# A relative-bias table built from 128 shifted copies of each row in DRAM, in a one-core decoder trunk

## What is computed

```python
for i in range(DEPTH):                       # DEPTH = 2
    y = swiglu(rms_norm(h, g[0]), ffn_w_gate[i, 0], ffn_w_up[i, 0], ffn_w_down[i, 0])
    h = h + 0.5 * rms_norm(y, g[1])
    u = rms_norm(h, g[2])
    y = nsa_mixer(u, ..., rel_bias) if i % 2 == 0 else fox_mixer(u, ...)
    h = h + rms_norm(y, g[3])
    y = swiglu(rms_norm(h, g[4]), ffn_w_gate[i, 1], ffn_w_up[i, 1], ffn_w_down[i, 1])
    h = h + 0.5 * rms_norm(y, g[5])
```

## Time and profile before

| | |
|---|---|
| median of 3 runs | 1093.38 us |
| profiled execution, its own time | 1094.15 us |
| its span | 1092.4 us |
| PE busy | 1062.8 us, 97% |
| DVE, ACT, POOL busy | 574.5, 482.5, 104.4 us |
| bytes moved by DMA | 187.79 MB |
| sub-layer 0 (first FFN) | about 0 to 217 us |

### The profile page before, as it was taken

The page is one execution under the profiler, slowest core; times in us unless marked ns, Lnnn a source line. Parts: engine busy times, 40 slices in busy tenths (PEclk is TensorE's granted clock), DMA queues, the critical chain, the costliest instruction groups (busy, mean ns, idle before and its releaser), DMA issues.

```text
span 1092.4 us, 18174 instructions
## 1 busy us (share of the span) xinstructions
PE 1062.8 (97%) x7545; PEld 973.8 (89%) x7545; DVE 574.5 (53%) x645; ACT 482.5 (44%) x613; POOL 104.4 (10%) x206
## 2 busy tenths in 40 slices
PE   6999999999989999999999999999999999999997
PEld 6998999899956789999998999999899779999996
DVE  4543444644387464444456445455645765544444
ACT  5435433553266353443445343344465644444432
POOL 0100000112045010000001000000114410000000
PEclk8999999999989999999999999999999999999999
DMA  9686556477300356656554655655554126555551
GB/s 279 221 291 228 173 174 196 149 251 231 118 1 1 116 185 201 191 170 200 170 191 160 225 166 180 195 188 183 190 166 163 62 88 218 187 192 186 169 183 39
DMA packets 137814, 187.79 MB, mean 172 GB/s; under 512 B 7249, under 2 KB 120102, under 8 KB 137766
## 3 DMA queue, kind: packets, MB, share of 16 engines
q1 hardware_dynamic: 133702, 172.86, 49.3%
q0 software_dynamic: 3920, 14.18, 3.9%
q10 hardware_dynamic: 144, 0.07, 0.0%
HBM read 184.45 MB, written 1.07 MB: 170 GB/s over the span
## 4 chain that ended last, share of the span: by engine, by line
PE 91%; DVE 4%; POOL 1%; ACT 1%; issue 1%; DMA 1%; DVEq 0%; SPq 0%; ACTq 0%
PE ps L928 88%; PE ps L1163 2%; DMA raw<-in_ffn_w_gate 1%; DVE normed L669 1%; POOL ms_half L338 1%; DVE normed L649 1%; ACT ps L459 1%; PE ps L1008 1%; POOL rstd L344 1%; DVE xlo L677 0%; DVE res L658 0%; DVE probT_buf L755 0%; POOL ms L342 0%; ACT whi L623 0%; DVE wlo L637 0%
## 5 line engine op out<-in xcount | busy, mean ns | idle before, releaser
L637 DVE TENSOR_TENSOR wlo<-raw,whi 128x2048 fp32r<-128x2048 f32 x156 | 358.1, 2295 | 322.3 <-ACT whi L439 322.3
L928 PE MATMUL ps<-xhi,whi 128*128 128x256 f32 x1536 | 435.6, 284 | 0.0
L928 PE MATMUL ps<-xhi,wlo 128*128 128x256 f32 x1536 | 434.7, 283 | 0.0
L928 PE MATMUL ps<-xlo,whi 128*128 128x256 f32 x1536 | 434.7, 283 | 0.0
L439 ACT ACTIVATE whi<-raw 128x2048 fp32r<-128x2048 f32 x156 | 297.6, 1908 | 112.1 <-PE ps L928 110.6
L928 PEld LDWEIGHTS ps<-xhi,whi 128*128 128x128 f32 x1536 | 294.6, 192 | 2.6 <-issue 1.2
L928 PEld LDWEIGHTS ps<-xlo,whi 128*128 128x128 f32 x1536 | 294.6, 192 | 1.6 <-issue 0.2
L928 PEld LDWEIGHTS ps<-xhi,wlo 128*128 128x128 f32 x1536 | 294.6, 192 | 0.0
L928 PE MATMUL ps<-whi,hhi 128*128 128x512 f32 x320 | 125.0, 391 | 0.0
L928 PE MATMUL ps<-wlo,hhi 128*128 128x512 f32 x320 | 125.0, 391 | 0.0
L928 PE MATMUL ps<-whi,hlo 128*128 128x512 f32 x320 | 124.5, 389 | 0.0
(11 more groups left out here) (167 smaller groups left out, 857.3 us busy)
## 6 DMA issues: line engine op xcount, KB each, us to landing
raw<-in_ffn_w_gate SPq DMA_DIRECT2D x44, 1024.0 KB, 5.4
raw<-in_ffn_w_up SPq DMA_DIRECT2D x44, 1024.0 KB, 5.4
raw<-in_ffn_w_down SPq DMA_DIRECT2D x44, 1024.0 KB, 4.9
raw<-in_fox_w_in SPq DMA_DIRECT2D x12, 1024.0 KB, 5.3
raw<-in_nsa_w_in SPq DMA_DIRECT2D x10, 1024.0 KB, 5.3
big<-in_nsa_cmp_w POOLq DMA_DIRECT2D x2, 2048.0 KB, 10.2
raw<-in_nsa_w_out SPq DMA_DIRECT2D x4, 1024.0 KB, 5.1
raw<-in_fox_w_out SPq DMA_DIRECT2D x4, 1024.0 KB, 4.9
```

Source lines behind the costliest of these rows:

```text
L637: nc.vector.tensor_tensor(wlo[:, slot, :], raw[:, slot, :], whi[:, slot, :].bitcast(F32), ALU.subtract).then_inc(w_lo, 1)
L928: return nc.tensor.matmul(out_, l, r, start=start, stop=stop)
```

## The change

`scratch` in DRAM grows from 16 x 384 to 16 x 128 x 385 float32. One DMA on POOL's queue now writes each of the 16 rows 128 times: its source is `vrev` with a step of zero over the copies, its destination 2048 pieces of 384 numbers (1536 bytes), 385 numbers apart, 3.15 MB in all. A second DMA reads `scratch` from element 127 on with a step of 384 from partition to partition, so that partition p gets the row shifted by 127 - p, in the right order of the queries, straight into `bias` (2048 rows of 1 KB, 2 MB, as the skewed read before). The reversed identity, the 8 matmuls, the 8 copies on ACT and their semaphores go. The load of `w1` stands right behind the write and ahead of the wait for it. Chunk 3 of the first FFN becomes the first turn of the loop. DVE waits for `bias_in` ahead of the first use of `bias`.

```diff
             pool.wait_ge(pre_evac, 1)
-            pool.dma_start(scratch, vrev[:, :]).then_inc(vrev_out, 16)
+            copies = vrev[:, :]
+            copies = bass.AP(copies.tensor, copies.offset, [list(copies.ap[0]), [0, P], [1, SCORES]])
+            pool.dma_start(bass.AP(scratch.tensor, 0, [[P * (SCORES + 1), H], [SCORES + 1, P], [1, SCORES]]), copies).then_inc(vrev_out, 16)
+            pool.dma_start(w1, cmp_w1[0, 0].rearrange("(k p) n -> p k n", p=P)).then_inc(w1_in[0], 16)
             pool.wait_ge(vrev_out, 16)
-            pool.dma_start(skew, bass.AP(scratch.tensor, 0, [[1, P], [SCORES, H], [1, S]])).then_inc(skew_in, 16)
+            pool.dma_start(bias[:, :, :], bass.AP(scratch.tensor, P - 1, [[SCORES, P], [P * (SCORES + 1), H], [1, S]])).then_inc(bias_in, 16)
             load_gain(0, 1)
             load_gain(1, 0)
-            pool.wait_ge(bias_mm, 8)
-            pool.dma_start(w1, cmp_w1[0, 0].rearrange("(k p) n -> p k n", p=P)).then_inc(w1_in[0], 16)
             between_sublayers(0)
...
-                    chunk(3)
-                    for k in range(8):
-                        act.wait_ge(bias_mm, k + 1)
-                        nc.scalar.activation(bias[:, 2 * k:2 * k + 2, :], ps[:, OB + k % 2, :].rearrange("p (a n) -> p a n", a=2),
-                                             ACT.Copy).then_inc(bias_ready, 1)
-                with act.Fori(4 if s == 0 else 2, NCH - 1) as c:
+                with act.Fori(3 if s == 0 else 2, NCH - 1) as c:
                     chunk(c)
...
+                        dve.wait_ge(bias_in, 16)
                         s_ = ps[:, OB, 0:TT * H * NC].rearrange("p (t h c) -> p t h c", t=TT, c=NC)
...
-                    chunk(3)
-
-                    pe.wait_ge(skew_in, 16)
-                    for k in range(8):
-                        if k >= 2:
-                            pe.wait_ge(bias_ready, k - 1)
-                        mm(ps[:, OB + k % 2, :], cst[:, C_J:C_J + P], skew[:, 2 * k:2 * k + 2, :], True, True).then_inc(bias_mm, 1)
-                with pe.Fori(4 if s == 0 else 2, NCH - 1) as c:
+                with pe.Fori(3 if s == 0 else 2, NCH - 1) as c:
                     chunk(c)
...
-    args.append(nc.dram_tensor("scratch", (H, SCORES), F32, kind="Internal").ap())
+    args.append(nc.dram_tensor("scratch", (H, P, SCORES + 1), F32, kind="Internal").ap())
```

More of the change, by code:

```diff
@@ L62 @@
 NORM = [(0, 0), (0, 2), (0, 4), (1, 0), (1, 2), (1, 4)]
-C_ID, C_J, C_MASK, C_VALID, C_A1, C_A2, C_R, C_NEG, C_SEL = 0, 128, 256, 512, 514, 530, 546, 548, 564
-C_END = 564 + P
+C_ID, C_MASK, C_VALID, C_A1, C_A2, C_R, C_NEG, C_SEL = 0, 128, 384, 386, 402, 418, 420, 436
+C_END = C_SEL + P
 GWC = 48 + 2 * H
@@ L81, in tables @@
     c[:, C_ID:C_ID + P] = np.eye(P)
-    c[:, C_J:C_J + P] = np.eye(P)[::-1]
     p, j = np.arange(P)[:, None], np.arange(S)[None, :]
@@ L130, in trunk @@
         big = sb("big", [P, 4096])
-        skew = big[:, :].rearrange("p (h n) -> p h n", h=H)
         w1 = big[:, :].rearrange("p (k n) -> p k n", k=16)
@@ L212, in trunk @@
         pre_mm, pre_evac = sem("pre_mm"), sem("pre_evac")
-        vrev_out, skew_in = sem("vrev_out"), sem("skew_in")
-        bias_mm, bias_ready = sem("bias_mm"), sem("bias_ready")
+        vrev_out, bias_in = sem("vrev_out"), sem("bias_in")
         proj_ready = sem("proj_ready")
@@ L708, in ffn @@
                     chunk(2)
-                    chunk(3)
-                with dve.Fori(4 if s == 0 else 2, NCH - 1) as c:
+                with dve.Fori(3 if s == 0 else 2, NCH - 1) as c:
                     chunk(c)
```

## The result

The changed kernel takes **1113.39 us** (median of 6 runs, 1112.98 to 1114.94), the one before 1093.88 us in the same set: the ratio over all runs is 1.0166, with a 95% interval of 1.0143 to 1.0190. By the medians it is 19.5 us slower. The forecast was 1111.0, between 1088 and 1125.

A forecast was written before the change was run, and what follows sets the result against it. PE, busy 97% of the span, was taken to bound the kernel if its weights arrive in time. 1093.4 - 7.15 (stage removed) + 17.0 (up stall) + 6.8 (gate stall) + 1.0 (clock) = 1111.0 us; range 1088 to 1125.

The forecast's parts named there:

- The gain, 7.15 us: PE's bias stage in the first FFN: without the 8 float32 matmuls, 7.15 us go from PE.
- The write's rate, 100 GB/s: POOL's write of 3.15 MB from 16 partitions: taken at 100 GB/s, 31.5 us, from 49.6 to 81.1.
- wide bounds: For the write's duration: 9.0 us at 348 GB/s on one side, 51 us at 62 GB/s on the other.
- Three pieces to a packet, one weight packet for each: POOL's and SP's queues: 1 KB of weights passes beside each 4.6 KB packet of the write, 22 GB/s for weights.
- Rival B: Slow write, but each 1.5 KB piece its own packet; weights get 67 GB/s, stalls 14.3 us, total 1100.6 us; chance 0.20.
- The up unit, 17.0 us: First FFN: up weights land at 88.5 us, PE starts at 92.7 instead of 75.75, standing for 17.0 us.
- I start at 55.3: Up unit's load: its data was taken to begin moving at 55.3 us, with 0.57 of 1.05 MB passed by 81.1.
- The gate unit, 6.8 us: First FFN: gate weights land near 101 us, PE can start at 105.2 after ending up at 98.4: 6.8 us more.
- The clock, 1.0 us: After PE's idling its granted clock falls to 0.50; between 0 and 3.1 us may be lost afterwards, 1 taken.
- Rival A: The write runs at full rate, 9 us; gate unit stalls 3 to 5 us, total 1089.3 to 1091.3 us; chance 0.18.
- the sign's turning point of about 280 GB/s: Write rate at or above which nothing is lost; the sign turns where PE's stalls reach 7.15 us.
- Rival C: The slow write holds up only POOL's queue, weights fare no worse; full gain, 1086.2 us; chance 0.10.

The follow-up runs named there:

- the paced versions: The changed kernel's 128-copy write cut into four DMAs released by waits on the weights' progress: 1086.99 us from vrev, 1086.64 us from a copy in DRAM.

## Why the prediction was right, step by step

- **The gain, 7.15 us.** Right: the paced versions get 1094 - 1086.8 = 7.2.
- **The write's rate, 100 GB/s.** Right: 101 GB/s, over after some 32 us (31.5 forecast). It was a choice between wide bounds, and its lower one was read a little off: behind the slice of 236 the row shows four slices of 62 to 92 GB/s, not five. The Trainium skill ("SBUF — State Buffer", Door 1: The DMA port swizzle) gives 104 GB/s for partitions 0 to 15; the long writes agree (101, 97), and the short pieces among the weights went faster (most of them 0.2 MB in 1.0 to 1.2 us), so there the measurement decides. The Trainium skill's rule that 512 B are enough for line rate ("DMA: Bandwidth & Descriptors", Specifications) agrees with the write from 128 partitions, 346 GB/s in pieces of 1.5 KB; for the narrow source the same pieces gave 101.
- **Three pieces to a packet, one weight packet for each.** Right: 4.6 KB, 259 against 260. Rival B falls for this kernel; on ACT's queue its condition holds, and its 1100.6 lies in that run's lower group, by luck: B had stalls at the gate unit and the next up unit, and the one stall there was at the up unit, 12.2 us, with 2.8 us for the clock.
- **The up unit, 17.0 us.** Measured 20.9. The step that was off is "I start at 55.3": its first packets came after 66 us, 13 us after the issue and not 2. So 0.35 instead of 0.57 MB had passed by the end of the write; the rest ran beside w1 as worked out. The sum itself has a small slip: 81.1 + 6.9 is 88.0 and not 88.5, which put the stall 0.5 us too high.
- **The gate unit, 6.8 us.** Measured 2.9 us of idling and 1.9 us by which the up unit ran slower before it: 4.8. It landed at 102.3, forecast 101; since the up unit was later, less was left to wait. The two errors offset each other. That is not luck alone: what ends the stall is the end of POOL's queue, and that was well placed.
- **The clock, 1.0 us.** Measured 1.7 after the second stall. Beside it, the up unit was to take 11 us at the lower clock and took 7.6, because the clock was back at 99.9 and not behind the unit.
- Sum of the delays: 20.9 + 4.8 + 1.7 = 27.4 against 24.8; total +20.2 in the profile against +17.6 forecast, 19.5 in the medians. The mechanism and the order of events were the forecast ones; the terms were each off by up to 4 us, in both directions.

Rival A (a write at full rate) is not this kernel, and its price was too low: with 128 partitions the lower group is at 1093.8 to 1094.3 against 1089.3 to 1091.3. The stall of 5.0 us lay within my 3 to 5, but at the up unit, which I had landing just in time (again the late first packet), and I had left out the clock, 2.8 us. With that falls the sign's turning point of about 280 GB/s: at 346 nothing was won. And a difference of 2.2 us, which I said a measurement can tell, is well inside the 7 us that the kernel before spreads over by itself. Rival C (a slow packet holds up only its own queue) is refuted for this kernel: no packet of weights moved for 13 us while the engines were held 96% by 101 GB/s. The runs with short pieces show a part of it after all (see the hardware below).

## What to carry to other kernels

A transfer that is "hidden" still takes turns with the stream that feeds the bound engine: count its packets beside the stream's, and compare how long its queue stays full with the slack of the next loads. Taking 7 us off the busiest engine paid in full here only when the traffic that replaced it came in short pieces, released by the progress of the stream itself. And look at the number of partitions at a transfer's SBUF end: 16 of them gave 101 GB/s in a long write, 128 gave 346.

## What the runs showed of the hardware

**A load issued behind slow packets waits before its first byte.** The up load's first packet moved 13.4 us after its issue when POOL's packets of 4.6 KB took 0.7 us each. In the kernel before it was 3.2 us, behind the fast write from 128 partitions 4.6, behind the copy from DRAM 7.8, behind the write on ACT's queue 11.4. In all of these 1.2 to 1.6 MB of other queues' work passed first, and its time depends on that work's speed. It is not particular to SP's loads: in the run on ACT's queue POOL's load of w1, issued at 48.30, moved its first packet at 63.8, behind 1.4 MB of the write. Why is not shown.

**The issuing engine can be held as well.** SP's issue of the third weight load, with two still waiting:

```profile
62.76 24.61 SPq L264 DMA_DIRECT2D raw<-in_ffn_w_down  x1
```

It took 24.6 us where the others take 0.37; in the run from 128 partitions it took 9.0, with four pieces 0.37. It cost nothing here, because SP's next load (96.11) had to wait for a slot of `raw` longer than that.

**A packet from the narrow source holds its engine for a time that depends on what ran before it.** In the long write a packet of 4.6 KB takes 0.70 us. Cut into 16 pieces, its 768 packets took 0.62 us on average in a full queue and 0.19 us when each piece came by itself among the weights. And where three queues took turns, on ACT's queue from 68 to 72 us, the engines moved 390 GB/s in all while the narrow write kept its 90:

```profile
DMA packets 701, 1.56 MB, mean 390 GB/s; under 512 B 0, under 2 KB 466, under 8 KB 701
...
q10 hardware_dynamic: 233, 0.36, 28.4%
```

So the narrow source need not cost the others their bandwidth; it did so in the long write, where each of its packets of 0.70 us had at most one weight packet of 1 KB for company.

**A stage that falls to the lower clock in some executions only.** The profile of the run in 16 paced pieces is of an execution of 1093.21 us, that of the run in four pieces of one of 1086.58. The same stretch of PE in both (us, busy, clock, DMA share, GB/s):

```profile
250.00:266.00 16.00, 16.00 (x87) 0.57 0.63 208
```

```profile
250.00:266.00 16.00, 16.00 (x140) 1.00 0.92 303
```

At 250 us PE begins the 60-column matmuls of the NSA compression after a wait of 0.5 us. In the first run the granted clock falls to 0.5 near 252 us for 14 us, in the second it does not fall; PE gets 87 matmuls done where it otherwise does 140. The run on ACT's queue and the one with one piece, profiled at 1106.56 and 1108.93 us, show the same fall at 267 us, in the same stage; the changed kernel and the kernel before do not show it in their profiles (1113.56 and 1094.15 us). Of the kernel before no execution near 1100 us was profiled, so there the cause is inferred: the 9 of 22 near 1100 us had a mean granted clock of 0.988, the 13 near 1094 one of 0.990 to 0.995. The fall is as large as the gain in question, and a median over few runs can fall on either side of it.
